# A diffusion trunk layer on one core: the first modulation in quarters, and its projection on two contraction tiles at a time

## The reference, cut to what matters

```python
cond = silu(c);  cond_ctx = silu(c_ctx)
m  = split(cond     @ mod_w + mod_b, 6)      # mod_w: 1024 x 6144
mc = split(cond_ctx @ mod_w + mod_b, 6)
h  = rms_norm(x,   norm1_g) * (1 + m[1])  + m[0]     # scale m[1], shift m[0]
hc = rms_norm(ctx, norm1_g) * (1 + mc[1]) + mc[0]
... = split(h @ w_in), split(hc @ w_in)      # w_in: 1024 x 6656
```

## Time and profile before

| | |
|---|---|
| runs, us | 864.87, 864.95, 863.32; median 864.87 |
| the profiled execution's own time, us | 862.41 |
| its span, us | 860.2 |
| TensorE (PE) busy, share of the span | 805.8 us, 94% |
| VectorE (DVE), ScalarE (ACT), GpSimd (POOL) busy | 405.1, 193.0, 116.5 us |
| mean granted clock of TensorE | 0.977 of full |
| read from HBM, written | 124.70 MB, 10.49 MB |

### The profile page before, as it was taken

One profiled execution on the slowest core, in us unless ns is written; L12 is line 12 of the kernel. 1 busy time (PEld: TensorE's weight loads), 2 busy tenths in 40 slices (PEclk: granted clock), 3 DMA queues, 4 the chain that ended last, 5 costly groups with the idle time before them and its releaser, 6 DMA issues.

```text
span 860.2 us, 9956 instructions
## 1 busy us (share of the span) xinstructions
PE 805.8 (94%) x3861; PEld 439.4 (51%) x3861; DVE 405.1 (47%) x873; ACT 193.0 (22%) x400; POOL 116.5 (14%) x103
## 2 busy tenths in 40 slices
PE   4999999999999999999999999999999668899994
PEld 3445466564574544555555555678544333344441
DVE  3219654575254432656557667652222663322221
ACT  4121256401001103222322323010013211121120
POOL 1000000000017720010110110111200012121212
PEclk9899999999999999999999999999999969999998
DMA  8961020120034303435235361602251579999934
GB/s 310 378 212 66 33 98 1 48 77 2 1 101 169 123 0 129 141 98 192 77 102 168 99 220 49 197 1 98 110 232 74 220 283 417 344 382 396 326 93 59
DMA packets 52071, 131.72 MB, mean 153 GB/s; under 512 B 8587, under 2 KB 9308, under 8 KB 47922
## 3 DMA queue, kind: packets, MB, share of 16 engines
q1 hardware_dynamic: 47698, 120.52, 38.3%
q0 software_dynamic: 3744, 8.40, 4.4%
q10 hardware_dynamic: 576, 2.10, 0.6%
HBM read 124.70 MB, written 10.49 MB: 157 GB/s over the span
## 4 chain that ended last, share of the span: by engine, by line
PE 91%; DMA 3%; DVE 3%; ACT 1%; issue 1%; POOL 0%; SPq 0%; POOLq 0%; DVEq 0%; ACTq 0%
PE ps L628 85%; PE ps L631 6%; DMA arena<-xd,tok_of 2%; DMA out<-arena,half_of 1%; ACT arena L1342 1%; DMA arena<-in_x 0%; DVE arena L2232 0%; ACT arena L1310 0%; DVE arena L1615 0%; POOL out L2431 0%; DVE arena L1666 0%; POOL stat L2369 0%; ACT arena L1539 0%; DVE arena L2106 0%; DVE arena L1610 0%
## 5 line engine op out<-in xcount | busy, mean ns | idle before, releaser
L628 PE MATMUL ps<-arena 128*128 128x512 f32 (+11 forms) x3098 | 723.8, 436 | 17.0 <-DVE arena L2075 4.7
L628 PEld LDWEIGHTS ps<-arena 128*128 128x128 f32 (+5 forms) x3098 | 355.5, 163 | 339.6 <-issue 315.3
L1342 ACT ACTIVATE arena<-ps 128x512 f32<-128x512 f32 (+5 forms) x132 | 55.6, 446 | 238.2 <-PE ps L628 150.3
L631 PE MATMUL ps<-tab,arena 128*128 128x128 f32 x436 | 62.2, 286 | 11.9 <-DVE arena L1615 6.6
L631 PEld LDWEIGHTS ps<-tab,arena 128*128 128x128 f32 x436 | 52.4, 148 | 39.4 <-issue 30.8
L2405 POOL TENSOR_TENSOR arena<-arena 128x512 f32<-128x512 f32 x24 | 31.7, 1320 | 273.1 <-DVE arena L1787 216.1
L2369 POOL TENSOR_TENSOR stat<-stat,mhalf 128x1 f32<-128x1 f32 (+2 forms) x20 | 23.2, 1160 | 317.8 <-DVE stat L1590 257.3
L1431 ACT ACTIVATE arena<-ps 128x512 f32<-128x512 f32 x24 | 14.3, 597 | 131.6 <-PE ps L628 131.6
L1755 DVE SCALAR_TENSOR_TENSOR arena<-arena,cond 128x512 f32<-128x512 f32 x56 | 42.6, 760 | 2.3 <-PE ps L631 0.6
L1787 DVE SCALAR_TENSOR_TENSOR arena<-arena,ps 128x512 f32<-128x512 f32 x24 | 16.5, 687 | 52.3 <-ACT arena L1431 52.1
L1925 DVE TENSOR_REDUCE stat<-ps 128x1 f32<-128x768 f32 (+2 forms) x32 | 27.4, 856 | 24.8 <-PE ps L628 24.3
(11 more groups left out here) (202 smaller groups left out, 413.0 us busy)
## 6 DMA issues: line engine op xcount, KB each, us to landing
arena<-in_moe_w SPq DMA_DIRECT2D x32, 1024.0 KB, 13.5
arena<-in_w_in SPq DMA_DIRECT2D x12, 2048.0 KB, 8.9
arena<-in_mod_w SPq DMA_DIRECT2D x16, 1024.0 KB, 5.2
arena<-in_moe_w SPq DMA_DIRECT2D x32, 512.0 KB, 13.9
arena<-in_mod_w SPq DMA_DIRECT2D x4, 2048.0 KB, 16.3
arena<-in_w_out SPq DMA_DIRECT2D x2, 2048.0 KB, 10.2
arena<-in_x SPq DMA_DIRECT2D x4, 512.0 KB, 5.3
arena<-in_w_in SPq DMA_DIRECT2D x2, 1024.0 KB, 17.7
```

The costliest lines, as they stand in the source:

```text
L628: return nc.tensor.matmul(o, l, r, start=start, stop=stop, skip_group_check=True)
L631: return nc.tensor.transpose(o, i, ident[0:n, 0:n])
L1342: return A_(o, i, ACT.Copy)
```

## The change

The four products are no longer shift and scale of one half each, but both of a quarter: product q makes shift and scale of contraction tiles 2q and 2q + 1, from 256 columns of the shift's weights and 256 of the scale's. So each product's weights come in two transfers of 1 MB with rows of 1 KB, and chunk 3 of `w_in` in four transfers of two contraction tiles each, one behind each product's weights (on the semaphores `first_rows_in`, `early_in[1]`, `ring_in[0]`, `ring_in[2]`). VectorE has four `quarter_mods` in place of two `half_mods`, each followed by two `modulate_x`. `proj_first(g, q)` does contraction tiles 2q and 2q + 1, for q = 0 to 2; `proj(g)` is left with tiles 6 and 7. TensorE's list is reordered so that a block of the projection stands between each of products 1 to 3 and its turn, and the context groups come after the token groups. On ScalarE the copy of product 2 moves ahead of the context's modulation.

```diff
--- before.py
+++ after.py
@@ -357,7 +357,7 @@
         mod_out, mod_back = sem("mod_out"), sem("mod_back")
         rowsT, small_ready, small_exp = sem("rowsT"), sem("small_ready"), sem("small_exp")
         a1_ready, ssq_done, xn_done = sem("a1_ready"), sem("ssq_done"), sem("xn_done")
-        early_in, first_half_in = [sem("early_in0"), sem("early_in1")], sem("first_half_in")
+        early_in, first_rows_in = [sem("early_in0"), sem("early_in1")], sem("first_rows_in")
         xT_done, raw_act, raw_dve, hT_x, hT_c, modc_step = sem("xT_done"), sem("raw_act"), sem("raw_dve"), sem("hT_x"), sem("hT_c"), sem("modc_step")
         pj_mm, pj_done, pool_set = sem("pj_mm"), sem("pj_done"), sem("pool_set")
         lb_zero, dve_step, act_step, pool_step = sem("lb_zero"), sem("dve_step"), sem("act_step"), sem("pool_step")
@@ -404,7 +404,7 @@
 
         def ring_value(n):
 
-            return sum((48 if LOADS[m][1] in (0, 2) else 32) if LOADS[m][0] == "gate" else 16 for m in range(n % RING, n + 1, RING))
+            return sum((48 if LOADS[m][1] in (0, 2) else 32) if LOADS[m][0] == "gate" else (48, 32)[m] if LOADS[m][0] == "mod" else 16 for m in range(n % RING, n + 1, RING))
 
         def used_value(n):
 
@@ -412,7 +412,6 @@
 
         gates = gate_steps()
         MODS = 8
-        FIRST_MODS = [0, 2, 1, 3]
 
         def proj_bank(g):
 
@@ -509,14 +508,25 @@
             cs = A["ctx"][0].rearrange("(t p) d -> t p d", p=P)
             for t in range(XT):
                 sp.dma_start(xin[:, t], xs[t]).then_inc(x_in[t], 16)
-            for a in range(2):
-                sp.dma_start(early[a], mw[:, :, 2 * a * CW:(2 * a + 1) * CW]).then_inc(early_in[a], 16)
-            sp.dma_start(ring[:, 2, 0:4, :], wi[:, 0:4, 3 * CW:4 * CW]).then_inc(first_half_in, 16)
+            QW = CW // 2
+
+            def load_mod_quarter(dst, q, ready):
+                sp.dma_start(dst[:, :, 0:QW], mw[:, :, q * QW:(q + 1) * QW]).then_inc(ready, 16)
+                sp.dma_start(dst[:, :, QW:CW], mw[:, :, D + q * QW:D + (q + 1) * QW]).then_inc(ready, 16)
+
+            def load_first_rows(q, ready):
+                sp.dma_start(ring[:, 2, 2 * q:2 * q + 2, :], wi[:, 2 * q:2 * q + 2, 3 * CW:4 * CW]).then_inc(ready, 16)
+
+            load_mod_quarter(early[0], 0, early_in[0])
+            load_first_rows(0, first_rows_in)
+            load_mod_quarter(early[1], 1, early_in[1])
+            load_first_rows(1, early_in[1])
             for t in range(XT, NT):
                 sp.dma_start(xin[:, t], cs[t - XT]).then_inc(x_in[t], 16)
-            load(0)
-            load(1)
-            sp.dma_start(ring[:, 2, 4:KD, :], wi[:, 4:KD, 3 * CW:4 * CW]).then_inc(ring_in[2], 16)
+            load_mod_quarter(ring[:, 0, 0:KD, :], 2, ring_in[0])
+            load_first_rows(2, ring_in[0])
+            load_mod_quarter(ring[:, 1, 0:KD, :], 3, ring_in[1])
+            load_first_rows(3, ring_in[2])
             sp.dma_start(tab[:, P:], A["table"][:, P:]).then_inc(table_in, 16)
             sp.dma_start(rope[:, :, :, :], A["rope"].rearrange("(t p) f -> p t f", p=P)
                          .rearrange("p t (a f) -> p t a f", a=2)).then_inc(small_in, 16)
@@ -649,7 +659,7 @@
             def first_mod(i):
 
                 if i < 2:
-                    pe.wait_ge(early_in[i], 16)
+                    pe.wait_ge(early_in[i], (32, 48)[i])
                     w = early[i]
                 else:
                     pe.wait_ge(ring_in[i - 2], ring_value(i - 2))
@@ -667,10 +677,10 @@
             def turn_mod(i):
 
                 pe.wait_ge(mrow_ready, i + 1)
-                if i == 2:
-                    pe.wait_ge(a1_ready, 1)
+                if i:
+                    pe.wait_ge(a1_ready, i)
                 for j in range(4):
-                    ct = 4 * FIRST_MODS[i] + j
+                    ct = KD * (j // 2) + 2 * i + j % 2
                     last = mm(ps[:, 7, 2 * ct:2 * ct + 2], mrow[:, i, j * P:(j + 1) * P], pick2[:, :], True, True)
                 last.then_inc(mrowT, 1)
 
@@ -679,8 +689,6 @@
                 turn_x(t)
             first_mod(0)
             turn_mod(0)
-            first_mod(1)
-            turn_mod(1)
 
             def mod_sum(m):
 
@@ -690,15 +698,15 @@
                 last.then_inc(macc_mm, 1)
 
 
-            def proj_first(g):
+            def proj_first(g, q):
 
                 n, c, kind, t = groups[g]
-                if g == 2:
-                    pe.wait_ge(first_half_in, 16)
-                if g == 0:
+                if g == 2 and q == 0:
+                    pe.wait_ge(first_rows_in, 16)
+                if g == 0 and q == 0:
                     pe.wait_ge(raw_act, NT)
                     pe.wait_ge(raw_dve, NT)
-                for k in range(4):
+                for k in range(2 * q, 2 * q + 2):
                     if g == 2:
                         pe.wait_ge(hT_x, k + 1)
                     if g == 0:
@@ -711,12 +719,12 @@
                 slot = n % RING
                 pe.wait_ge(ring_in[slot], ring_value(n))
                 if g in (6, 7):
-                    pe.wait_ge(a1_ready, 2)
+                    pe.wait_ge(a1_ready, 4)
                 if g >= 8:
                     pe.wait_ge(pj_done, g - 1)
                 bank = proj_bank(g)
                 lo, hi = {0: (256, 512), 2: (0, 256), 4: (0, 256)}.get(c, (0, 512)) if t >= XT else {1: (256, 512)}.get(c, (0, 512))
-                for k in range(4 if g < NT else 0, KD):
+                for k in range(6 if g < NT else 0, KD):
                     w = ring[:, slot, k, :]
                     if g == 0:
                         pe.wait_ge(hT_c, k + 1)
@@ -885,18 +893,29 @@
                     last = turn(ps[:, bank, t * P:(t + 1) * P], yG[:, t, ft * P:(ft + 1) * P])
                 last.then_inc(yT_mm, 1)
 
-            proj_first(2)
-            proj_first(3)
+            proj_first(2, 0)
+            proj_first(3, 0)
+            first_mod(1)
+            proj_first(4, 0)
+            turn_mod(1)
+            proj_first(5, 0)
+            proj_first(2, 1)
             turn_x(4)
-            proj_first(4)
+            proj_first(3, 1)
             turn_x(5)
-            proj_first(5)
             first_mod(2)
+            proj_first(4, 1)
             turn_mod(2)
-            proj_first(0)
+            proj_first(5, 1)
+            proj_first(2, 2)
+            proj_first(3, 2)
             first_mod(3)
+            proj_first(4, 2)
             turn_mod(3)
-            proj_first(1)
+            proj_first(5, 2)
+            for g in range(2):
+                for q in range(3):
+                    proj_first(g, q)
             for g in range(12):
                 proj(g)
             pe.wait_ge(table_in, 16)
@@ -1324,13 +1343,13 @@
             sum_squares(5)
             raw_x(4)
             raw_x(5)
-            act.wait_ge(a1_ready, 1)
+            mod_rows(2)
+            act.wait_ge(a1_ready, 2)
             act.wait_ge(raw_act, NT)
             for k in range(4):
                 modulate_ctx(k)
-            mod_rows(2)
             mod_rows(3)
-            act.wait_ge(a1_ready, 2)
+            act.wait_ge(a1_ready, 4)
             act.wait_ge(raw_dve, NT)
             for k in range(4, KD):
                 modulate_ctx(k)
@@ -1614,19 +1633,19 @@
                 rsqrt(stat[:, t:t + 1], stat[:, t:t + 1], 1.0 / D)
                 V.tensor_scalar(xin[:, t], xin[:, t], stat[:, t:t + 1], None, ALU.mult).then_inc(xn_done, 1)
 
-            def half_mods(half):
-
-                dve.wait_ge(mrowT, 2 * half + 2)
+            def quarter_mods(q):
+
+                dve.wait_ge(mrowT, q + 1)
                 got = ps[:, 7, 0:32].rearrange("p (c s) -> p c s", s=2)
-                c = slice(4 * half, 4 * half + 4)
-                c8 = slice(8 + 4 * half, 12 + 4 * half)
-                V.tensor_tensor(modc[:, c, :], got[:, c, :], cols[:, 16 + 4 * half:20 + 4 * half].unsqueeze(2).broadcast_to([P, 4, 2]), ALU.add)
-                V.tensor_tensor(modc[:, c8, :], got[:, c8, :], cols[:, 24 + 4 * half:28 + 4 * half].unsqueeze(2).broadcast_to([P, 4, 2]),
+                c = slice(2 * q, 2 * q + 2)
+                c8 = slice(KD + 2 * q, KD + 2 * q + 2)
+                V.tensor_tensor(modc[:, c, :], got[:, c, :], cols[:, 16 + 2 * q:18 + 2 * q].unsqueeze(2).broadcast_to([P, 2, 2]), ALU.add)
+                V.tensor_tensor(modc[:, c8, :], got[:, c8, :], cols[:, 24 + 2 * q:26 + 2 * q].unsqueeze(2).broadcast_to([P, 2, 2]),
                                 ALU.add).then_inc(modc_step, 1)
-                dve.wait_ge(modc_step, half + 1)
-                V.scalar_tensor_tensor(A1[:, c, :], modc[:, c8, :], 1.0, cols[:, 64 + 4 * half:68 + 4 * half].unsqueeze(2).broadcast_to([P, 4, 2]),
+                dve.wait_ge(modc_step, q + 1)
+                V.scalar_tensor_tensor(A1[:, c, :], modc[:, c8, :], 1.0, cols[:, 64 + 2 * q:66 + 2 * q].unsqueeze(2).broadcast_to([P, 2, 2]),
                                        ALU.add, ALU.mult).then_inc(a1_ready, 1)
```

(20 more changed lines are left out.)

## The result

The changed kernel took 856.51 us (median of 5, 855.84 to 858.72), the kernel before 863.32 beside it (median of 5): ratio 0.9915, interval 0.9899 to 0.9932. Two more measurements of the same pair gave 0.9928 (0.9901 to 0.9954) and 0.9938 (0.9912 to 0.9963). The medians lie 6.6 to 7.0 us apart in the three measurements, the means over all runs 6.2; 2.25 were forecast, and 856.51 lies under the range (860.3 to 865.0).

The account below looks back on a forecast made before the run. TensorE (PE 91% of the span) was taken as the bound. Queue terms 3.62 - 2.83 + 0.86 = 1.65 us plus 0.6 from the clock made 2.25, so 864.87 - 2.25 = 862.6 us; range 860.3 to 865.0.

Parts of the forecast that it names:

- The start of the projection: TensorE's first projection matmul no longer waits behind the second product: at 23.49 instead of 27.11, 3.62 us earlier.
- the three terms: TensorE's queue: 3.62 us earlier start, less 2.83 for second product and turn moved behind it, plus 0.86 for copies: 1.65.
- The covers: Projection blocks between product and turn hide ScalarE's copy: 0.72 us for the second product, net 0.43 each for three and four.
- The clock: TensorE's low-clock stretch at the projection's start was expected to remain, somewhat shorter: 0.6 us taken as gain.
- more from the clock: Rival: denser TensorE queue makes the low-clock stretch short or missing; 2.9 to 4.6 us gained, say 861.2; chance 0.20.
- VectorE's spares: VectorE's extra small operations stay hidden, with 0.35 us spare at the modulate and 0.2 at the context's normalise; cost 0.
- the freed slot: After products three and four TensorE still waits for its own product to end before freeing the ring slot: 0.29 us each.
- VectorE kept its slack: Downstream, VectorE stands 1.12 us for ScalarE at 96.15 and longer later, so what the front wins goes to the end.
- The price of the thinner rows: DMA packets of 1 KB take 48 ns by interpolation, so a product's 2 MB takes 5.9 us instead of 5.4.
- the cover of 1.5 us: First product starts at 17.93 behind TensorE's transposes, leaving 1.5 us to hide 0.5 us more of weight loading.
- The slower rival: 1 KB packets cost the same 88 ns as 2 KB ones, so products' weights come late: 872.7 us; chance 0.10.
- decision point of 71 ns: Weight loading: kernel slower than before from 3.3 us more per product, 71 ns a packet.

Follow-up runs that it names:

- the kernel before without its second wait: Kernel before, second product made from the first product's weights, so it waits for none of its own (output differs): 860.35 us, ratio 0.9956.
- opening the covers: Changed kernel with each turn right behind its product again, the projection block between them moved behind the turn: 861.54 us, ratio 0.9969.
- the copies covered: Kernel before, products 3 and 4 separated from their turns by the context's projection block: 863.97 us, ratio 1.0002.
- the gap filled: Kernel before with six small identity matmuls in TensorE's gaps around the second turn: 860.51 us, ratio 0.9970.
- the held start: Changed kernel, projection's first block made to wait also for the second product's weights (semaphore also counts w_in's second pair): 861.67 us, ratio 0.9982.

## Why the prediction was wrong

**In short.** Against the kernel before without its second wait, the changed kernel gains 2.5 us: 1.86 without the clock and 0.7 by the clock, where 1.65 and 0.6 were forecast. What the prediction put at nothing is that wait, worth 3.7 us: 1.75 by itself and 2.0 by the low time that comes with it.

**The start of the projection.** "So it starts at 23.49, 3.62 us earlier": 23.11 measured, and 22.40 and 23.97 in the two other profiles. The working itself holds: from the first turn to the projection the kernel without the second wait takes 25.64 - 19.75 = 5.89 us, the changed kernel 22.40 - 20.16 = 2.24, which is 3.65 apart. The place was right, the difference was not. It was taken against 27.11, which belonged to an execution whose early low clock had already made the first product late. Where the early clock is high, the kernel before waits 1.72 us for the second product's weights and does not start sooner for it, while the changed kernel does. That is the missed term, 1.75 us (the kernel before without that wait, clock taken out). The earlier trace rows held it: the weights landed at 21.8, and the second product started at 22.21, 0.4 us of cover that I did not read as a bound.

**The queue.** Without the clock the changed kernel stands 1.86 us under the kernel that has the old order but no second wait (3.61 - 1.75). The sum of the three terms was 1.65. From the first turn to the next chunk the two profiles give the same: 81.00 - 21.23 = 59.77, less 2.95 for the low clock, against 76.10 - 20.86 = 55.24, a difference of 1.58. The covers: 1.6 expected, 1.8 measured when taken away.

**The clock.** 0.6 us was taken, between rows of one execution. Measured: 7.1 us less low time per run, 2.6 us. This is the term that was mis-sized. The step that failed is "after a like stretch of little work, so I expect it low": the stretch is not alike, for the kernel before has the wait for weights in it, and the gap of 0.72 behind three products. Taking away the one wait lowered the low time by 5.3 us; putting a wait of 4.77 us into the changed kernel raised it by 4.7; opening the covers raised it by 4.7. That the remaining 0.7 us agree with the 0.6 taken is partly luck: 0.6 was a choice between two rows of one execution. The Trainium skill, page "TensorE: Matmul & The Clock Gate", section "What's actually happening", had it that the low stretch would differ from run to run. The runs agree: 31 to 52 us per run in the kernel before, and in the windows from 14 to 36 us a mean clock of 1.00, 0.92 and 0.84 in the three profiles of the changed kernel. The rival "more from the clock" (856.51 is below its 860.3 too) named the mechanism, but not the wait that went with it.

**What held.** 1.86 + 1.75 + 2.6 make the 6.2 us between the means. VectorE's spares sufficed: TensorE waits neither for the normalise nor for a modulate after 23.11. Products 3 and 4 have their copies covered; the freed slot costs 0.14 us on the chain (40.47, 50.50), as against 0.29 taken. VectorE kept its slack: the wait of 1.12 us at 96.15 is gone, and the next one, 4.33 us long in the kernel before (103.02), is 2.54 (98.12). The price of the thinner rows came out near the interpolation: 692 packets in 2 us at a share of 110.1% are 51 ns each, 48 were worked out. But the cover of 1.5 us, of which 1.0 was to be left, was not there: the first product's weights landed at 18.2 in the first profile (issued at 5.6, 12.6 us to landing) where 16.9 was worked out, and at the high clock the transposes ended at 17.57, so the product waited 0.65. In the two other profiles they landed at 17.5. Single landings move by such amounts: with the order of before they come at 16.4 to 17.2 in five profiles. The second pair of `w_in`'s rows came 1.5 us later than worked out, of which 1.3 had gathered by the first product. The slower rival did not happen; its decision point of 71 ns was not reached. The Trainium skill's page "DMA: Bandwidth & Descriptors" (section "Anatomy of one DMA") has a fixed part of 2.0 us for each transfer, told there of the GpSimd path; paid in series it would have put the first weights at 16.9 + 2.0 = 18.9 (a wait of 1.0 us by the prediction's start of 17.93, and not the 0.5 written there, which left the thinner rows out). The landings at 18.2, 17.5 and 17.5 lie below, and with rows of 2 KB in the same number of transfers the first product did not wait at all (17.09).

**What stays open.** The fit gives 0.37 us of time for each us of low time, where dense work alone would give 0.50, probably since part of the low time falls where TensorE waits anyway; that was not tested. How much of the 2.6 lies in the front was not measured run by run; each measurement has one trace. The traces put it there: from 14 to 36 us the mean clock is 0.77 in both profiles that have the kernel before unaltered there (its own, and that with the copies covered), which is 10.1 us of low time, and 1.00, 0.92 and 0.84 in the three of the changed kernel, on average 3.5. From 670 to 740 us, in the mixture of experts, all of these five have 0.83 to 0.85, 21 to 24 us of low time, which the change does not touch.

## What to carry to other kernels

A wait that one profile does not show may only be hidden by another delay in front of it: list when each transfer lands beside when its user asks, and treat a margin of a few tenths as a bound that appears once the work before it gets quicker. Where TensorE works at the beginning in short bursts, size a change by the runs' mean clocks as well: executions of the kernel before lay up to 6.9 us apart (860.28 to 867.20), and longer with more low time. Work in smaller pieces pays when it lets the dense part begin on the first of its inputs, and leaves a block to put behind each hand-over.

## What the runs showed of the hardware

Being busy did not bring the clock back in one case, the slowest execution of its kernel: with the gap filled, TensorE was at work from 22.64 on, with a product, turns, identity matmuls and then dense projection, and the granted clock stayed at the lower level until about 34.8 (1.2 GHz). Two windows of that kernel, columns as in the earlier trace rows; in both PE is busy all the time:

```profile
27.00:28.00 1.00, 1.00 (x8) 1.00 (x6) 0.00 (x0) 0.98 (x2) 0.00 (x0) 0.50 1.05 391
...
34.00:35.00 1.00, 1.00 (x3) 0.45 (x2) 0.31 (x1) 0.00 (x0) 0.00 (x0) 0.58 0.99 375
```

A filler that runs at the low clock costs up to twice its price (1.22 us for the first four instructions there, 0.61 for four in the profiles with a high clock) and sits ahead of the work it was to help: the projection began at 30.64 there.

TensorE's clock fell while it stood for a transfer: 0.60 in the window from 21 to 22 us in the same profile, within the wait of 1.72 us, and 0.69 and 0.50 from 22 to 26 in the wait of 4.77 us of the held start. In the profile of the kernel before without the wait for the second product's weights it stayed at 1.00 from 8 to 80 us.

Rows of 1 KB went at about 350 GB/s over the 16 engines (348 from 20 to 22 us of the changed kernel) where rows of 2 KB went at 388 (the same stretch of the kernel before), and the share of engine time was 110% against 105%.
